# Seven block products for the feed-forward output matrix as well, and where VectorE makes the sums they need

## The reference, cut to what matters

```python
def swiglu(x, w_in, w_out):
    a, b = jnp.split(x @ w_in, 2, axis=-1)
    return (jax.nn.silu(a) * b) @ w_out
for l in range(DEPTH):
    h = h + 0.5 * swiglu(rmsnorm(h, ffn1_norm[l]), ffn1_w_in[l], ffn1_w_out[l])
    ...   # projections, sparse attention, pooling, attention into 256 memory tokens, gates
    h = h + merged @ w_out[l]
    h = h + 0.5 * swiglu(rmsnorm(h, ffn2_norm[l]), ffn2_w_in[l], ffn2_w_out[l])
return rmsnorm(h, final_norm)
```

## Time and profile before

| | us |
|---|---|
| median of 3 runs (2153.53 to 2153.96) | 2153.89 |
| the profiled execution's own time | 2153.99 |
| its span, first to last instruction | 2152.2 |
| TensorE busy | 2130.2 (99%) |
| VectorE busy | 1373.7 (64%) |
| GpSimd busy | 1380.6 (64%) |
| ScalarE busy | 882.2 (41%) |

### The profile page before, as it was taken

How to read it: one execution, slowest core, us unless ns; L and a number is a source line. 1 busy time by engine, 2 the same in 40 slices (tenths; PEclk the granted TensorE clock), 3 DMA queues, 4 the chain that set the end, 5 groups by cost and what they waited for, 6 DMA issues and landing times.

```text
span 2152.2 us, 36180 instructions
## 1 busy us (share of the span) xinstructions
PE 2130.2 (99%) x12838; PEld 1881.5 (87%) x12838; DVE 1373.7 (64%) x2582; ACT 882.2 (41%) x1717; POOL 1380.6 (64%) x1030
## 2 busy tenths in 40 slices
PE   9999999999999999999999999999999999999997
PEld 7998998878888899899889899888888888998996
DVE  6763886578754577177568448746877456752863
ACT  5532532544553354054145235225445533531541
POOL 6776778644446667587667667785444374876773
PEclk9999999999999999999999999999999999999999
DMA  5343333222213223333333433342122132333332
GB/s 171 107 156 97 106 96 122 96 69 65 74 54 103 98 89 99 98 104 99 107 101 118 133 98 104 101 130 79 64 74 69 48 119 79 104 101 95 115 95 82
DMA packets 90028, 210.81 MB, mean 98 GB/s; under 512 B 9824, under 2 KB 13064, under 8 KB 89608
## 3 DMA queue, kind: packets, MB, share of 16 engines
q1 hardware_dynamic: 85680, 203.32, 29.5%
q10 hardware_dynamic: 4184, 5.31, 0.8%
HBM read 206.48 MB, written 3.68 MB: 98 GB/s over the span
## 4 chain that ended last, share of the span: by engine, by line
PE 92%; DVE 5%; ACT 2%; issue 1%; DMA 0%; ACTq 0%; DVEq 0%; SPq 0%
PE bank L869 17%; PE bank L870 17%; PE bank L871 17%; PE bank L1005 11%; PE bank L1007 11%; PE bank L1006 11%; PE tbank L1222 1%; DVE mem L2040 1%; DVE yL L2048 1%; DVE bank L2015 1%; ACT u1H L1554 1%; DVE h L2020 1%; PE obank L1268 0%; DVE ssq L2023 0%; DVE bank L2030 0%
## 5 line engine op out<-in xcount | busy, mean ns | idle before, releaser
L741 POOL TENSOR_TENSOR wL<-raw,wH 128x1024 fp32r<-128x1024 f32 (+3 forms) x280 | 548.8, 1960 | 23.4
L738 POOL TENSOR_SCALAR wH<-raw 128x1024 fp32r<-128x1024 f32 (+3 forms) x280 | 248.3, 887 | 487.5 <-PE bank L871 421.0
L1005 PE MATMUL bank<-u1H,wH 128*128 128x256 f32 x1152 | 326.4, 283 | 3.3 <-DVE hidL L1940 3.3
L1006 PE MATMUL bank<-u1H,wL 128*128 128x256 f32 x1152 | 326.0, 283 | 0.0
L1007 PE MATMUL bank<-u1L,wH 128*128 128x256 f32 x1152 | 326.0, 283 | 0.0
L869 PE MATMUL bank<-u1H,wH 128*128 128x512 f32 x704 | 281.6, 400 | 0.0
L870 PE MATMUL bank<-u1H,wL 128*128 128x512 f32 x704 | 274.9, 391 | 0.0
L871 PE MATMUL bank<-u1L,wH 128*128 128x512 f32 x704 | 274.8, 390 | 0.0
L869 PE MATMUL bank<-hidH,wH 128*128 128x512 f32 x704 | 274.4, 390 | 0.0
L870 PE MATMUL bank<-hidH,wL 128*128 128x512 f32 x704 | 274.0, 389 | 0.0
L871 PE MATMUL bank<-hidL,wH 128*128 128x512 f32 x704 | 273.9, 389 | 0.0
(11 more groups left out here) (291 smaller groups left out, 4731.9 us busy)
## 6 DMA issues: line engine op xcount, KB each, us to landing
raw<-in_wA SPq DMA_DIRECT2D x296, 256.0 KB, 3.1
raw<-in_wM SPq DMA_DIRECT2D x96, 512.0 KB, 3.3
raw<-in_wB SPq DMA_DIRECT2D x64, 384.0 KB, 3.1
raw<-in_wB SPq DMA_DIRECT2D x64, 320.0 KB, 2.9
raw<-in_wA SPq DMA_DIRECT2D x28, 512.0 KB, 3.3
raw<-in_wR SPq DMA_DIRECT2D x32, 256.0 KB, 2.6
mem<-in_memT SPq DMA_DIRECT2D x2, 1024.0 KB, 7.9
near_bias<-bias_rows ACTq DMA_DIRECT2D x2, 1024.0 KB, 6.6
```

The costliest lines, as they stand in the source:

```text
L738: pool.tensor_scalar(wH[:, w, 0:cols], raw[:, slot, 0:cols], 1.0, 0.0, ALU.mult, ALU.add).then_inc(rounded, 1)
L741: pool.tensor_tensor(wL[:, w, 0:cols], raw[:, slot, 0:cols], wH[:, w, 0:cols].bitcast(F32), ALU.subtract).then_inc(split_done, 1)
L1005: pe.matmul(dst, a, hi, start=begin and k == 0, stop=False)
L1006: pe.matmul(dst, b, hi, start=False, stop=False)
```

## The change

The same `w_out` product is now made of seven block products for 16 of the 22 hidden tiles. The tiles are in three groups: A and B of eight, C of six (`GROUPS`). The order of pairs in a feed-forward block (`FLOW`) is: four S and four K pairs of A, one K pair of C, four O pairs of A (each makes two output tiles from the eight hidden tiles of A, by the same seven products and the same code as a K pair), eight K pairs of B, one of C, four O pairs of B, four K pairs of C. Then `outs` runs the standard product over the six tiles of C for the 8 output tiles (6 x 3 matmuls of 512 columns).

The O pairs need the sums and differences of blocks of hidden tiles: tiles t and t+4 of a group are a "couple" and give two rows of sums of 512, four instructions of 256 columns on VectorE (`couple_sums`). The gated result now goes to `keep` in SBUF instead of staying in PSUM; the sums read `keep`, and so does the low part. ScalarE rounds the sums (`couple_highs`), GpSimd makes their low parts (`couple_lows`). `add_rows` adds an O pair's two tiles into h. C pairs and O pairs are scaled by rms one at a time (`gate`, `add_rows`), so the last rows are not. The squares of memory tokens are added up inside the O windows from pieces of `memT` loaded into `keep`, and memT is loaded whole before the fifth C pair. Scaling of the memory tokens and their low parts stand behind the first and the second of the last rows (`norm_mem`, `low_mem`). Loading `near_bias` moves behind the last rows.

The diff, cut to what the prediction speaks of (PE, ScalarE and SyncE code that only follows the new order is left out):

```diff
-HALF = (12, 10)
-
+GROUPS = {"A": (0, 8), "B": (8, 8), "C": (16, 6)}
+COUPLES = (0, 4, 1, 5, 2, 6, 3, 7)
...
+    order = [("S", "A", t) for t in COUPLES[:4]] + [("K", "A", t) for t in COUPLES[4:]]
+    order += [("K", "C", 0)] + [("O", "A", i) for i in range(4)]
+    order += [("K", "B", t) for t in COUPLES] + [("K", "C", 1)] + [("O", "B", i) for i in range(4)]
+    order += [("K", "C", t) for t in range(2, N_OUT)]
...
+            if p.at < 4:
+                return near4H[:, p.at, :], near4L[:, p.at, :]
+            return far4H[:, p.at - 4, :], far4L[:, p.at - 4, :]
+        def kept(p):
...
+                def load_mem_piece(group):
+                    last = pair_of("K", group, 7)
+                    sp.wait_ge(pair_done, k_at(l, 0, last) + 1)
+                    sp.wait_ge(couple_sum, 4 * couple_at(ffn_at(l, 0), last) + 4)
+                    n = 4 * N_GROUP[group]
+                    sp.dma_start(mem_piece[:, :, :], memT[:, n:n + 4, :]).then_inc(mem_piece_landed, 16)
...
+                def couple_lows(f, p):
+                    c, j = couple_at(ffn_at(l, f), p), p.at % 4
+                    for i, r in enumerate((2 * j + 1, 2 * j)):
+                        pool.wait_ge(couple_sum, 4 * c + 4)
+                        pool.wait_ge(couple_high, 2 * c + i + 1)
+                        pool.tensor_tensor(sumL[:, r, :], sumS[:, r, :], sumH[:, r, :].bitcast(F32), ALU.subtract
+                                           ).then_inc(couple_low, 1)
...
+                    def couple_highs(p):
+                        c, j = couple_at(ffn_at(l, f), p), p.at % 4
+                        for i, r in enumerate((2 * j + 1, 2 * j)):
+                            act.wait_ge(couple_sum, 4 * c + 3 + i)
+                            act.activation(sumH[:, r, :], sumS[:, r, :], ACT.Copy).then_inc(couple_high, 1)
...
+                    def add_rows(p):
+                        g = k_at(l, f, p)
+                        dve.wait_ge(crossed, g + 1)
+                        own.done(dve.tensor_tensor(bank[3][:, :], bank[3][:, :], rms[:, :], ALU.mult))
+                        own.wait()
+                        for i, made in ((0, obank), (1, bank[3])):
+                            row = h[:, 2 * p.at + i, :]
+                            own.done(dve.scalar_tensor_tensor(row, made[:, :], 0.5, row, ALU.mult, ALU.add))
+                        own.wait()
+                        dve.sem_inc(pair_done, 1)
                     def gate(p):
+                        dst = bank[3][:, :] if p.group == "C" else kept(p)
+                        if p.group != "C":
+                            dve.wait_ge(couple_sum, 4 * couple_at(ffn_at(l, f), p) + int(p.at >= 4))
...
                         if p.kind == "K":
-                            g = k_at(l, f, p)
+                            g, n = k_at(l, f, p), hid_at(l, f, p)
                             dve.wait_ge(crossed, g + 1)
+                            dve.wait_ge(k_scaled, n + 1)
                             own.done(dve.tensor_tensor(bank[3][:, :], bank[3][:, :], ta[:, :], ALU.mult))
                             own.wait()
-                            dve.wait_ge(k_sigmoid, g + 1)
-                            dve.tensor_tensor(bank[3][:, :], bank[3][:, :], sg[:, 0, :], ALU.mult).then_inc(k_gated, 1)
+                            if p.group == "C":
+                                own.done(dve.tensor_tensor(bank[3][:, :], bank[3][:, :], rms[:, :], ALU.mult))
+                                own.wait()
+                            dve.wait_ge(k_sigmoid, n + 1)
+                            dve.tensor_tensor(dst, bank[3][:, :], sg[:, 0, :], ALU.mult).then_inc(k_gated, 1)
                             return
...
                     def low(p):
+                        hi, lo = hidden_row(p)
+                        src = (bank[3] if p.group == "C" else kept(p))[:, 0:hi.shape[-1]]
                         if p.kind == "K":
-                            dve.wait_ge(k_high, k_at(l, f, p) + 1)
-                            dve.tensor_tensor(hidL[:, p.pos, :], bank[3][:, :], hidH[:, p.pos, :].bitcast(F32),
-                                              ALU.subtract).then_inc(pair_done, 1)
+                            dve.wait_ge(k_high, hid_at(l, f, p) + 1)
...
+                    def couple_sums(p):
+                        c, j = couple_at(ffn_at(l, f), p), p.at % 4
+                        left, right = slice(0, TH), slice(TH, T)
+                        if p.at < 4:
+                            dve.tensor_tensor(sumS[:, 2 * j, left], keep[:, 0, right], keep[:, 0, left], ALU.subtract
+                                              ).then_inc(couple_sum, 1)
+                            return
+                        dve.tensor_tensor(sumS[:, 2 * j + 1, right], keep[:, 1, right], keep[:, 0, right], ALU.subtract
+                                          ).then_inc(couple_sum, 1)
+                        dve.tensor_tensor(sumS[:, 2 * j + 1, left], keep[:, 1, right], sumS[:, 2 * j, left], ALU.subtract
+                                          ).then_inc(couple_sum, 1)
+                        dve.wait_ge(couple_sum, 4 * c + 3)
+                        dve.tensor_tensor(sumS[:, 2 * j, right], keep[:, 1, left], sumS[:, 2 * j + 1, left], ALU.subtract
+                                          ).then_inc(couple_sum, 1)
...
+                        if seven_then:
                             low_s2(then)
-                        if k_now:
+                        if last is not None and last.kind == "O" and f == 0:
+                            add_mem(last)
+                        if seven_now:
                             mix_two(now)
-
+                        if last is not None and in_couple(last):
+                            couple_sums(last)
...
-                def last_half(unit, n_from, g, hi, lo):
-                    own.restart()
+                def last_row(k, unit, n_from, g, hi, lo):
+                    dve.wait_ge(unit_used, unit_at(l, unit + OUT_UNIT + k))
+                    finish_h(k, bank[k % BANKS][:, :], sbank[k % 2][:, :], 0.5, l * 24 + k + (n_from + 1), g, hi, lo)
+                def norm_mem():
+                    inverse_rms(l * 5 + 2, mem_rms[:, :], M)
+                    dve.wait_ge(mem_loaded, l * 16 + 16)
...
-                        ps = bank[k % BANKS][:, :]
-                        dve.wait_ge(unit_used, unit_at(l, unit + OUT_UNIT[1] + 2 * k + 1))
-                        own.done(dve.tensor_tensor(ps, ps, rms[:, :], ALU.mult))
-                        own.wait()
-                        finish_h(k, ps, sbank[k % 2][:, :], 0.5, l * 24 + k + (n_from + 1), g, hi, lo)
-                    own.restart()
+                        ins = dve.tensor_tensor(mem[:, k, :], mem[:, k, :], mem_rms[:, :], ALU.mult)
+                        if k < KD - 1:
+                            own.done(ins)
+                        else:
+                            ins.then_inc(mem_normed, 1)
...
+                def low_mem():
+                    for k in range(KD):
+                        dve.wait_ge(mem_high, l * KD + (k + 1))
+                        dve.scalar_tensor_tensor(mem_lo[:, k, :], mem[:, k, :], pr[:, G_MEM + k:G_MEM + k + 1],
+                                                 mem_hi[:, k, :].bitcast(F32), ALU.mult, ALU.subtract
+                                                 ).then_inc(mem_ready, 1)
 
                 ffn(0, 1)
 
-                dve.wait_ge(mem_loaded, l * 16 + 16)
...
-                for k in range(KD):
-                    ins = dve.tensor_tensor(mem[:, k, :], mem[:, k, :], mem_rms[:, :], ALU.mult)
-                    if k < KD - 1:
...
                 dve.wait_ge(par_loaded, l * 16 + 16)
                 for k in range(KD):
-                    dve.wait_ge(mem_high, l * KD + (k + 1))
...
-                last_half(0, 8, G_MIX, u1H, u1L)
+                    last_row(k, 0, 8, G_MIX, u1H, u1L)
+                    if k == 0:
+                        norm_mem()
+                    if k == 1:
+                        low_mem()
+                own.restart()
```

More of the change, by code:

```diff
@@ new lines, in lay_pairs, with pair_of, in_couple, couple_at @@
+    return flow, count["S"], count["7"], hid, unit
+FLOW, N_S, N_K, N_HID, OUT_UNIT = lay_pairs()
+OUT_CHUNK = OUT_UNIT
+U_FFN = C_FFN = OUT_UNIT + KD
+N_GROUP = {"A": 0, "B": 1}
+assert N_K % 2 == 0 and U_FFN % 4 == 0
+def pair_of(kind, group, at):
+    return next(p for p in FLOW if p.group == group and p.at == at and (p.kind == "O") == (kind == "O"))
+def in_couple(p):
+    return p.kind != "O" and p.group in "AB"
+def couple_at(ffn, p):
+    return ffn * 8 + N_GROUP[p.group] * 4 + p.at % 4
@@ L699, in layer @@
+                    for q in ("A11", "A12", "A21", "A22"):
+                        quarters_free(q, last_k(l, f))
+                    units(wC, 16, KD * f, KD, N_OUT * P, unit + OUT_UNIT)
                 ffn_units(0)
@@ L1027, in seven_products @@
                         pe.wait_ge(pool_low, pool_lows_to(g, "A12"))
```

(8 more changed lines are left out.)

512 lines of the change are left out of this document (252 added, 260 removed).

## The result

The changed kernel takes 2213.11 us (median of 4 runs, 2210.12 to 2215.44), the kernel before 2153.93 (4 runs): a ratio of 1.0274, 95% interval 1.0256 to 1.0292. It is 59 us slower. The forecast was 2260 us, within 2185 to 2320, and slower: the direction and the range held, but the slowdown forecast was nearly double the measured one.

The account below looks back on a forecast made before the run. The prediction took TensorE to bound the kernel, busy 2130 of 2152 us, with VectorE full in K windows. Its terms: 2154.0 - 25.6 + 80 + 2 + 40 + 5 + 4 = 2259.4, rounded to 2260 us, range 2185 to 2320.

Parts of the forecast that it names:

- TensorE's gain: Matmuls in all four feed-forward blocks: eight O pairs per block replace the standard product over 16 tiles, 25.6 us less.
- The couples: VectorE in the 24 couples among K pairs: each 3.05 us over TensorE's pace, 73 us more.
- the 23.2 forecast: VectorE's time for a couple's two windows: 20.06 us, 2.7 of waits for GpSimd and 0.46 for a later sigmoid.
- Rival 1: K windows: waits of two-SBUF instructions are small because VectorE's and GpSimd's orders miss each other; 2179 us, chance 0.14.
- The hand-overs' 14 us: Eight hand-overs to O pairs: the last couple's low parts come about 1.8 us late each, 14 us more.
- The O windows: O pairs in a layer's first block: one two-SBUF addition of memory squares each, +1 us a block, 2 in all.
- My own test: Signs in the profile after: wrong if sums run at 0.36 to 0.42, TensorE doesn't wait at ends, or O pairs are slower.
- C windows: C pairs: one more scaling of 0.73 us on VectorE, mostly hidden by existing waits; nothing worth a term.
- The ends: Last rows of each layer's first block: VectorE's chain ends 20 us after TensorE's 45.0, +40 us for two.
- The second block: Last rows of layer one's second block: high parts come late for the next product, +5 us.
- The 2 us a layer for transfers: Loading memory tokens between the weight quarters of K pairs and between O pairs: 2 us a layer, +4 us.
- Rival 4: Block ends: TensorE's waits drop its clock, up to 6 us lost at each of four; 2275 to 2284 us, chance 0.11.

Follow-up runs that it names:

- the three edits together: Changed kernel with memory-token squares added on GpSimd, sums ahead with the second tile in PSUM, and last rows interleaved: 2152.10 us, 0.9991 of the kernel before.

## Why the prediction was right in sign and off in size

**TensorE's gain** was right: O pairs run at 10.08 us where VectorE leaves them alone (the later O windows of the second blocks), rows at 0.227 us a matmul.

**The couples** are the step that was mis-sized: "six such instructions ... I take 6 x 0.45 = 2.7 us". The mechanism is shown by the pair of runs with one order and different memories. The size is 1.4 us per couple (0.7 in the four sums, 0.7 in the two low parts), since three sums in a row are one exposure, not three: the first waits for GpSimd's instruction, and there is none behind it. I had multiplied the mean wait of the earlier trace rows, where GpSimd always had a next instruction. That is 1.3 of the 1.7 us between the 23.2 forecast and the 21.47 measured: 24 couples are 31 us over TensorE's pace, where the forecast had 73. Rival 1 (waits so small that the couples cost nothing, 2179 us) was 34 us off on the other side, nearer than the forecast's 47; its mechanism fails by the waits in the rows. The hand-overs' 14 us came out, 13.7, but not by the path that I gave: only 3.2 us of it are waits for the low parts (L859), the rest is mostly waits for banks that VectorE frees late (L1959, L1982).

**The O windows** were wrong, in the term I had put at 2 us: "one addition of memory squares with two SBUF inputs, 0.8 against 0.6 of slack". I took the same mean for a place where the order of both engines repeats exactly, and the addition always falls on GpSimd's low part of S1, here as VectorE's and GpSimd's rows have it:

```profile
146.78 1.31 DVE L2057 TENSOR_TENSOR mem_rms<-keep,mem_rms 128x256 f32<-128x256 f32 x1
```
```profile
146.51 1.29 POOL L836 TENSOR_TENSOR wL<-wS,wH 128x512 fp32r<-128x512 f32 x1 [0.63 <-ACT wH L1497]
```

It costs 1.31 + 0.14, the slack is 10.08 - 9.7 = 0.4, and 16 windows give 17 us. In the first window of a layer a copy stands in place of the addition, with one input in SBUF and its output there too, and it is almost as long:

```profile
135.77 1.18 DVE L2054 COPY mem_rms<-keep 128x256 f32<-128x256 f32 x1
```

So I can't say that only two SBUF inputs make an instruction wait; no run shows this copy with GpSimd idle. My own test said that I am wrong if O pairs are slower than K pairs: in the first blocks they are, 11.13 against 10.7. C windows, which I put at nothing, take VectorE 10.35 us, but TensorE loses nothing in them where VectorE comes in time (second blocks, and all blocks with the squares on GpSimd); they only keep it from making up for the O windows.

How near the forecast came owes something to luck: the missed 17 us made up for part of what the couples didn't cost. Against the run that moves the squares (2199.5 us, 46 over before) the forecast's slowdown of 106 would be 2.3 times the measured one, in place of 1.8.

**The ends** were right in kind and place; the chain is 53.7 us long from 341.1 (last square at 394.76) where I laid out 59.4. Rows take 4.14 us for 4.47, and the low parts 3.24 for 6.1, without a wait, because GpSimd itself waited for TensorE. Measured 29.4 for 40. The second block: 4.2 for 5. The 2 us a layer for transfers are not found as a wait of their own.

**Rival 4** was real, at about half its price. The granted clock over stretches of the changed kernel (window: length, PE, PEld, DVE, ACT, POOL busy; PEclk, DMA share, GB/s):

```profile
63.20:69.90 6.70, 6.08 (x28) 6.08 (x29) 4.46 (x8) 2.38 (x4) 5.59 (x6) 0.50 0.31 88
341.00:362.00 21.00, 21.00 (x95) 17.24 (x93) 14.74 (x23) 4.70 (x7) 15.45 (x11) 1.00 0.38 119
367.00:370.30 3.30, 3.30 (x9) 2.60 (x8) 3.30 (x9) 2.26 (x6) 0.00 (x0) 0.50 0.49 159
370.30:376.00 5.70, 4.37 (x19) 3.26 (x18) 3.38 (x6) 1.98 (x3) 3.45 (x2) 1.00 0.00 0
394.10:397.60 3.50, 3.50 (x19) 3.50 (x18) 2.02 (x4) 1.91 (x2) 0.00 (x0) 0.50 0.87 297
1111.00:1114.40 3.40, 3.40 (x10) 2.65 (x9) 2.03 (x4) 1.66 (x3) 1.56 (x2) 0.50 0.42 118
```

Behind the waits of 3.24 and 5.22 us it stands at 0.50, 1.2 GHz, for 3.3 and 3.5 us; matmuls of 512 columns step by 0.43 in place of 0.227 us; then it is back at 1.00. The Trainium skill, "TensorE: Matmul & The Clock Gate", Part 1, says that an idle TensorE drops to 1.2 GHz; the trace agrees. That is 1.7 us twice in this end, 3.4 of the 15 lost there. The first and the last row show two more such places, in the first K pair of the launch (behind a wait of 2.73 us) and at the end of layer one's second block (behind 2.23 us); with the end in layer two there are six. By the matmuls' steps above 0.120 and 0.227 us they cost 11 us together, an estimate; before, no such stretch lies ahead of the launch's last 10 us. The prediction's sum had no term for it and rival 4 had up to 24, at the blocks' ends only. The 11 us are no addition to the table: they lie inside its rows. The last rows interleaved bring them to 6, the three edits together to 3, so part of what those edits gain is the clock's.

## What to carry to other kernels

Before an instruction with two SBUF inputs goes on VectorE, look at what GpSimd does at that very place: the price is what is left of its instruction, so count exposures in the two orders and don't multiply a mean. Keep one input in PSUM, and in these runs it is never paid; merge many such instructions into one, and it is paid at most once, or GpSimd's next instruction pays. And when a change shortens TensorE's share of a stretch, add up what other engines still have to do in it.

## What was not expected of the hardware

The same eight low parts of 128x256 took 3.24 us with GpSimd waiting for TensorE, and 8.39 and 13.81 us with GpSimd busy; as one subtraction over 128x2048, with the gain applied by ScalarE, they took 2.28 us. In a run of sums one waited for the rest of one GpSimd instruction and the following for nearly the whole of the next (0.91, then 1.51 us), while with a PSUM input 24 of 24 took 0.41 us in the same place. And it goes both ways: behind the start of a long instruction of VectorE with two SBUF inputs, GpSimd's took 2.68 us for 1.05.
